# A sparse-expert block whose router reads raw rows, with its adaptive sums placed elsewhere

## The chip, the cores and the metric

The kernel runs on one core of one Trainium2 chip. The metric is the device time of one execution in microseconds (us). The core has five engines that run their own instruction lists side by side and meet at semaphores: TensorE (PE in the profile; PEld is its weight load), VectorE (DVE), ScalarE (ACT), GpSimd (POOL) and SyncE (SP), which here issues most transfers. Each list is executed in order, so an instruction that waits holds back everything behind it on its engine.

## What is computed

Two blocks over 256 tokens of width 1024, in float32. The first is a mixer of three branches followed by a layer of experts; the second is four further layers, whose norms are modulated by adaptive rows (a vector `c` times a matrix plus a bias). The change lies in the first block and in the part of the adaptive rows that is computed during it. The expert layer:

```python
h = rms_norm(x, norm_ffn)                       # x * rsqrt(mean(x*x) + 1e-6) * norm_ffn
lg = h @ w_rg + b_rg;  grp = argmax(lg)         # 4 groups
le = (h @ w_re + b_re)[group grp]               # 8 experts in the group
top_p, top_i = top_k(softmax(le), 2)
gate = top_p / sum(top_p) * softmax(lg)[grp]
x = x + sum over both: gate * (silu(h @ w_eg[e]) * (h @ w_eu[e])) @ w_ed[e]
```

## The kernel before, in words

The program goes stage by stage; the end of a stage is a barrier of all engines. The first block is `hybrid_block` (norm, projections, `delta_rule`, `sparse_attention`, `mix_out`), then `moe_block`, which is `route` (L1386) and `experts` (L1903); `second_block` follows. Matrices are multiplied as high and low halves: ScalarE rounds a weight piece to the high half (`Stream.lift`, L276), VectorE subtracts it for the low half (`Stream.lower`, L286), TensorE makes three products (`product`, L314 to L316). SyncE sends piece n when the piece that had its slot has been lowered (`Stream.send`, L254). The experts' weights go through five slots of 1 MB.

`route` in its order before. SyncE: the norm's gain as 128 full rows, four small loads of the router's weights and biases, three weight pieces, three column loads for the adaptive rows; then, after the logits, bias rows. TensorE first sums the adaptive rows over the partitions: 16 products with a single column of ones, each behind one stir (L322, a dummy product), then turns the normed rows (L1456), makes the logits (L1465, 16 products of 36 columns), sums three half rows of 512 columns (L1353), stirs eight times, waits for the picked group, makes the ranks (L1475, L1478), stirs eight times, and gathers the tokens of each group with a permutation matrix (L1488: for each of eight column blocks the high and the low part in a bank of its own), then the tokens that overflow a group (L1495), then turns the permutation (L1502) and gathers the factors (L1506). ScalarE squares the rows (L1515), rounds the normed rows (L1519), copies half of the turned rows (L1521). VectorE norms the rows with the gain (L1547, that is why everything waits for the gain and the root of GpSimd, L1448), adds the biases (L1568), picks the group by some eight tiny steps, goes on to both experts, and only then waits for the ranks (L1585) and builds the permutation (L1589); then come the weights, the flag of overflow, the merge of the adaptive columns (L1333 to L1337) and the copies of the low halves (L1611). Row merges (`SiteRow.merge`, L1366) each wait for a bias load that overwrites the summed row; the last of them, whose sum and load follow the factors, is the last work of the stage.

`experts`: every engine first reads the flag (`first_of`, L1664), then runs 32 experts; at the end of each, `turn` waits for the product (L1953) and `down` waits for the low half of the hidden rows (L2073). `mix_out`: after the last branch TensorE turns the merged rows in two halves of eight (L3176); the second half waits for the merge of VectorE (L2290).

## Time and profile before

| what | value |
|---|---|
| time, median of 3 runs (lowest, highest) | 2376.83 us (2376.19, 2380.12) |
| span of the profiled execution | 2380.9 us |
| busy: TensorE, its weight load, VectorE, ScalarE, GpSimd | 95%, 80%, 76%, 48%, 6% |
| `route`: first instruction of TensorE to first product of the experts | 434.49 to 484.66 us |
| experts: first product to the turn of the last expert | 484.66 to 1032.22 us |

A row in order of time has the start, the duration, the engine, the line, output and inputs, and in brackets how long the engine sat idle before it and what released it. A float32 product stands as two records (so x16 is eight products), a product of rounded halves or a transposition as one. PEclk is the share of full speed that TensorE's clock was granted: 1.00 is 2.4 GHz and 0.50 is 1.2 GHz.

### The profile page before, as it was taken

How to read it: one execution, taken by the hardware profiler on the slowest of the kernel's cores; microseconds unless marked ns; L12 is line 12 of the kernel's file. 1: busy time of each engine (PE TensorE's matmuls, PEld its weight loads, DVE VectorE, ACT ScalarE, POOL GpSimd, SP SyncE). 2: the span in 40 equal slices, each digit the busy share in tenths (PEclk: the TensorE clock that was granted, in tenths of full speed). 3: DMA queues.
4: the chain of work that ended last, by engine and by line, in shares of the span. 5: the costliest groups of instructions: out<-in, count | busy, mean ns of one | idle time of the engine just before them, and what ended most of it. 6: DMA issues, size and time to landing. Idle time of an engine off the chain costs nothing. (4 is left out here: it accounts for less than half of the span.)

```text
span 2380.9 us, 30361 instructions
## 1 busy us (share of the span) xinstructions
PE 2265.6 (95%) x11981; PEld 1913.7 (80%) x11981; DVE 1813.5 (76%) x2133; ACT 1150.8 (48%) x1197; POOL 132.0 (6%) x229
## 2 busy tenths in 40 slices
PE   7999888999999999989999989999998999898997
PEld 7888677878888888878788887888987888797886
DVE  6887686478888888866788777887796888777545
ACT  4443244367767676744443254432653434364332
POOL 2000100000000000000111000110001111000000
PEclk9999988899999999999999999999999999999999
DMA  8844552489999999964699634996543898344662
GB/s 299 283 124 131 174 176 89 114 300 373 370 356 371 356 369 363 364 211 156 180 376 366 220 125 134 371 371 221 174 136 124 283 376 313 121 143 154 191 193 71
DMA packets 347057, 572.51 MB, mean 240 GB/s; under 512 B 68128, under 2 KB 181280, under 8 KB 346912
## 3 DMA queue, kind: packets, MB, share of 16 engines
q1 hardware_dynamic: 326176, 495.02, 61.5%
q0 software_dynamic: 20736, 75.51, 8.4%
q8 instruction: 97, 1.59, 0.3%
q14 instruction: 48, 0.39, 0.1%
HBM read 569.39 MB, written 1.05 MB: 240 GB/s over the span
## 5 line engine op out<-in xcount | busy, mean ns | idle before, releaser
L286 DVE TENSOR_TENSOR st_lo<-st_raw,st_hi 128x2048 fp32r<-128x2048 f32 (+1 forms) x195 | 441.0, 2267 | 117.5 <-ACT st_hi L276 117.2
L286 DVE TENSOR_TENSOR es_lo<-es_raw,es_hi 128x2048 fp32r<-128x2048 f32 x192 | 429.3, 2286 | 75.9 <-ACT es_hi L276 74.6
L276 ACT CAST st_hi<-st_raw 128x2048 fp32r<-128x2048 f32 (+1 forms) x195 | 368.4, 1892 | 232.5 <-PE ps L316 157.4
L314 PE MATMUL ps<-st_hi,sb_h_hi 128*128 128x512 f32 (+1 forms) x1232 | 462.9, 376 | 15.7 <-DVE sb_h_lo L1139 7.9
L316 PE MATMUL ps<-st_hi,sb_h_lo 128*128 128x512 f32 (+1 forms) x1232 | 453.1, 368 | 0.0
L315 PE MATMUL ps<-st_lo,sb_h_hi 128*128 128x512 f32 (+1 forms) x1232 | 452.9, 368 | 0.0
L276 ACT CAST es_hi<-es_raw 128x2048 fp32r<-128x2048 f32 x192 | 357.6, 1910 | 52.5 <-DMA es_raw<-in_w_expert_up_dram 25.5
L314 PEld LDWEIGHTS ps<-st_hi,sb_h_hi 128*128 128x128 f32 x1232 | 234.1, 190 | 58.4 <-issue 13.0
L316 PEld LDWEIGHTS ps<-st_hi,sb_h_lo 128*128 128x128 f32 x1232 | 233.9, 190 | 38.7
L315 PEld LDWEIGHTS ps<-st_lo,sb_h_hi 128*128 128x128 f32 x1232 | 234.4, 190 | 35.4
L314 PE MATMUL ps<-es_hi,moe_hg_hi 128*128 128x512 f32 x512 | 205.7, 402 | 5.1 <-PEq L61 5.1
L315 PE MATMUL ps<-es_lo,moe_hg_hi 128*128 128x512 f32 x512 | 202.6, 396 | 0.0
L316 PE MATMUL ps<-es_hi,moe_hg_lo 128*128 128x512 f32 x512 | 202.5, 395 | 0.0
L276 ACT CAST hs_hi<-hs_raw 128x1024 fp32r<-128x1024 f32 (+2 forms) x86 | 86.4, 1010 | 156.1 <-PE ps L316 90.1
L1190 DVE SCALAR_TENSOR_TENSOR t_ada<-t_aw,c,t_ada 128x1024 f32<-128x1024 f32 x126 | 156.7, 1279 | 0.4 <-DMA t_aw<-in_ada_w_dram 0.4
L286 DVE TENSOR_TENSOR hs_lo<-hs_raw,hs_hi 128x1024 fp32r<-128x1024 f32 (+2 forms) x86 | 100.7, 1177 | 54.2 <-ACT hs_hi L276 54.1
L314 PE MATMUL ps<-st_hi,t_hid_hi 128*128 128x512 f32 x352 | 140.4, 399 | 1.4 <-DVE t_hid_lo L1162 1.4
L316 PE MATMUL ps<-st_hi,t_hid_lo 128*128 128x512 f32 x352 | 137.2, 390 | 0.0
L315 PE MATMUL ps<-st_lo,t_hid_hi 128*128 128x512 f32 x352 | 137.0, 389 | 0.0
L314 PEld LDWEIGHTS ps<-es_hi,moe_hg_hi 128*128 128x128 f32 x512 | 96.4, 188 | 28.6 <-issue 6.6
L316 PEld LDWEIGHTS ps<-es_hi,moe_hg_lo 128*128 128x128 f32 x512 | 96.2, 188 | 23.6
L315 PEld LDWEIGHTS ps<-es_lo,moe_hg_hi 128*128 128x128 f32 x512 | 96.6, 189 | 22.0
(690 smaller groups left out, 3769.0 us busy)
## 6 DMA issues: line engine op xcount, KB each, us to landing
st_raw<-in_ffn_w_in_dram SPq DMA_DIRECT2D x176, 512.0 KB, 6.7
t_aw<-in_ada_w_dram POOLq DMA_DIRECT2D x144, 512.0 KB, 7.0
es_raw<-in_w_expert_gate_dram SPq DMA_DIRECT2D x64, 1024.0 KB, 8.2
es_raw<-in_w_expert_up_dram SPq DMA_DIRECT2D x64, 1024.0 KB, 7.4
es_raw<-in_w_expert_down_dram SPq DMA_DIRECT2D x64, 1024.0 KB, 7.3
st_raw<-in_ffn_w_out_dram SPq DMA_DIRECT2D x44, 1024.0 KB, 9.1
fb_aw<-in_ada_w_dram SPq DMA_DIRECT2D x39, 512.0 KB, 5.8
hs_raw<-in_w_in_dram SPq DMA_DIRECT2D x36, 512.0 KB, 7.3
```

The costliest lines, as they stand in the source:

```text
L276: act.copy(p.at(self.hi[:, m % self.held, :]), p.at(self.raw[:, n % self.slots, :])).then_inc(self.high, 1)
L286: dve.tensor_tensor(p.at(self.lo[:, m % self.held, :]), p.at(self.raw[:, n % self.slots, :]), p.at(self.hi[:, m % self.held, :]).bitcast(F ...
L314: pe.matmul(out, a_hi, b_hi, start=start, stop=False, skip_group_check=True)
L315: pe.matmul(out, a_hi, b_lo, start=False, stop=False, skip_group_check=True)
L316: return pe.matmul(out, a_lo, b_hi, start=False, stop=stop, skip_group_check=True)
L1190: op = dve.scalar_tensor_tensor(at, aw[:, m % 4, :], k.c[:, kb:kb + 1], at, ALU.mult, ALU.add)
```

## The change

Routing works on the raw rows: TensorE turns `X` itself from the stage's start; the root (1/rms, still from GpSimd) multiplies the logits per token, and the norm's gain is folded into the router's weights beforehand (a product on VectorE in `mix_out`) and into the gathered columns, where a partition is a feature. High and low parts are gathered into one bank and split again. Permutation and ranks come right behind the group's choice, ahead of the choice of experts. The factors are gathered as rounded halves. The small loads go to the start of `delta_rule`; the three weight pieces are the first loads of `route`. The stirs, except two, are gone; the single-column sums stand behind the logits and behind the ranks. The row sums go to `mix_out` (between the two halves of the turns, with a wait for ScalarE's copy) and to the end of `experts`; their biases are added on one partition by accumulating transfers of GpSimd ahead of the sums. The flag and the column merge go to experts 2 and 3, the reading of the flag to expert 8 on VectorE and ScalarE, to the end on TensorE and SyncE.

```diff
 
-    def sums(self, pe, stirs=0):
+    def sums(self, pe, a):
         pe.wait_ge(self.ada.added, self.ada.total)
-        for i in range(16):
-            stir(self.k, pe, 0, stirs)
-            last = pe.matmul(self.psum[:, i:i + 1], self.ada.thirds[i // 8][:, i % 8 * P:(i % 8 + 1) * P],
...
         @block.sync
         def _(sp):
-            with nc.allow_non_contiguous_dma("small vectors"):
-                sp.dma_start(gain[:], rows(A["norm_ffn"][0])).then_inc(q["gained"], 16)
-                for dst, src in smalls:
-                    sp.dma_start(dst, src).then_inc(q["small"], 16)
             S.send(sp, lent)
-            mod.load(sp)
+            sp.wait_ge(q["squared"], NT)
+            S.send(sp, lent + 1)
             sp.wait_ge(q["logits"], 1)
-            for c in range(2):
-                mine_row.load(sp, c)
-            next_row.load(sp, 0)
-            sp.wait_ge(q["low"], NT)
-            S.send(sp, S.slots)
-            next_row.load(sp, 1)
+            S.send(sp, S.slots + 1)
...
-            mod.sums(pe, 1)
-            for t in range(NT):
-                pe.wait_ge(q["normed"], t + 1)
+            for t in range(NT):
                 for i in range(8):
-                    last = pe.transpose(ps[:, 2 * t + i // 4, i % 4 * P:(i % 4 + 1) * P], h[:, t, i * P:(i + 1) * P],
+                    last = pe.transpose(ps[:, 2 * t + i // 4, i % 4 * P:(i % 4 + 1) * P], X[:, t, i * P:(i + 1) * P],
                                         k.ident[:])
                     if i % 4 == 3:
...
-            pe.wait_ge(q["small"], 16 * len(smalls))
+            stir(k, pe, 5, 2)
...
             last.then_inc(q["logits"], 1)
-            for c in range(2):
-                mine_row.sum(pe, c)
-            next_row.sum(pe, 0)
-            stir(k, pe, 0, 8)
+            M.site.sums(pe, 0)
...
             last.then_inc(q["ranked"], 1)
-            stir(k, pe, 0, 8)
+            M.site.sums(pe, 1)
             pe.wait_ge(q["high"], NT)
             pe.wait_ge(q["low"], NT)
             pe.wait_ge(q["placed"], 1)
-            for n, (w, i) in enumerate(jobs):
-                if n >= 4:
-                    pe.wait_ge(q["g_hi" if w == 0 else "g_lo"], n // 2 - 1)
+            for i in range(8):
+                if i >= 4:
+                    pe.wait_ge(q["g_lo"], i - 3)
+                for w in range(2):
+                    for t in range(NT):
+                        last = pe.matmul(ps[:, i % 4, :], (h_hi, h_lo)[w][:, t, i * P:(i + 1) * P],
+                                         perm[:, t, 0:NG, :].rearrange("p j s -> p (j s)"), start=w == t == 0,
+                                         stop=w == 1 and t == NT - 1)
+                last.then_inc(q["gathered"], 1)
+            for j in range(NJ):
                 for t in range(NT):
-                    last = pe.matmul(ps[:, n % 4, :], (h_hi, h_lo)[w][:, t, i * P:(i + 1) * P],
-                                     perm[:, t, 0:NG, :].rearrange("p j s -> p (j s)"), start=t == 0, stop=t == NT - 1)
-                last.then_inc(q["gathered"], 1)
...
+                    last = pe.transpose(ps[:, 4 + j // 2, j % 2 * T + t * P:j % 2 * T + (t + 1) * P],
+                                        perm[:, t, j, :].bitcast(F32), k.ident[:])
+            last.then_inc(q["turned_perm"], 1)
             for c in range(2):
                 for w in range(2):
-                    pe.wait_ge(q["g_hi" if w == 0 else "g_lo"], 7 + c)
+                    pe.wait_ge(q["g_lo"], 5 + 2 * c + w)
...
             pe.wait_ge(q["weighted"], 1)
...
+                    last = pe.matmul(turned_fac[:, j], perm[:, t, j, :], halves[:, t], start=t == 0, stop=t == NT - 1)
             last.then_inc(q["turned_perm"], 1)
-            pe.wait_ge(next_row.merged, 1)
-            next_row.sum(pe, 1)
...
             for t in range(NT):
-                act.wait_ge(q["normed"], t + 1)
-                act.copy(h_hi[:, t, :], h[:, t, :]).then_inc(q["high"], 1)
                 act.wait_ge(q["turned"], 2 * t + 1)
                 act.copy(hT[:, 0:4, t * P:(t + 1) * P], ps[:, 2 * t, :].rearrange("p (k s) -> p k s", k=4)
                          ).then_inc(q["copied0"], 1)
+            for t in range(NT):
+                act.wait_ge(q["rooted"], t + 1)
+                act.activation(h_hi[:, t, :], X[:, t, :], ACT.Copy, scale=ss[:, t:t + 1]).then_inc(q["high"], 1)
+            S.lift(act, 3)
             act.wait_ge(q["chosen"], 1)
             act.activation(ex[:], ex[:], ACT.Exp).then_inc(q["raised"], 1)
-            S.lift(act, 1)
-            for n, (w, i) in enumerate(jobs):
...
+            for i in range(8):
+                act.wait_ge(q["gathered"], i + 1)
+                act.activation(M.hg_hi[:, 0:NG, i, :], ps[:, i % 4, :].rearrange("p (j s) -> p j s", j=NG), ACT.Copy,
+                               scale=k.wgain[:, i:i + 1]).then_inc(q["g_hi"], 1)
             act.wait_ge(q["turned_perm"], 1)
             act.copy(M.permT[:].rearrange("p j t -> p (j t)"), ps[:, 4:6, :].rearrange("p b n -> p (b n)"))
+            for n in range(4):
+                act.wait_ge(q["late_done"], n + 1)
+                act.copy((M.hg_hi, M.hg_lo)[n % 2][:, NG, n // 2 * 4:n // 2 * 4 + 4, :].rearrange("p k s -> p (k s)"),
+                         ps[:, n, :])
...
-            dve.wait_ge(q["gained"], 16)
-            for t in range(NT):
-                dve.wait_ge(q["rooted"], t + 1)
-                dve.scalar_tensor_tensor(h[:, t, :], X[:, t, :], ss[:, t:t + 1], gain[:], ALU.mult, ALU.mult
-                                         ).then_inc(q["normed"], 1)
-            for t in range(NT):
                 dve.wait_ge(q["turned"], 2 * t + 2)
                 dve.tensor_copy(hT[:, 4:8, t * P:(t + 1) * P], ps[:, 2 * t + 1, :].rearrange("p (k s) -> p k s", k=4)
                                 ).then_inc(q["copied1"], 1)
             for t in range(NT):
                 dve.wait_ge(q["high"], t + 1)
-                dve.tensor_tensor(h_lo[:, t, :], h[:, t, :], h_hi[:, t, :].bitcast(F32), ALU.subtract
-                                  ).then_inc(q["low"], 1)
+                dve.scalar_tensor_tensor(h_lo[:, t, :], X[:, t, :], ss[:, t:t + 1], h_hi[:, t, :].bitcast(F32), ALU.mult,
+                                         ALU.subtract).then_inc(q["low"], 1)
...
             dve.wait_ge(q["logits"], 1)
-            after(dve.tensor_tensor(lt[:], ps[:, 4, 0:NT * 36].rearrange("p (t n) -> p t n", t=NT),
-                                    br[:].unsqueeze(1).to_broadcast([P, NT, 36]), ALU.add))
+            for t in range(NT):
+                op = dve.scalar_tensor_tensor(lt[:, t, :], logit(t), ss[:, t:t + 1], br[:], ALU.mult, ALU.add)
...
+            dve.wait_ge(q["ranked"], 1)
+            after(dve.tensor_tensor(cum[:], ranks[:, 0:NT, :], pick[:], ALU.mult))
+            after(dve.tensor_reduce(b1[:], cum[:], AX.X, ALU.add))
+            dve.tensor_scalar(rk[:, :, 0:NG], cum[:], -1.0, None, ALU.add)
+            after(dve.tensor_scalar(rk[:, :, NG:].rearrange("p t o -> p (t o)"), b1[:], -1.0 - P, None, ALU.add))
+            dve.tensor_tensor(perm[:].rearrange("p t j s -> p (t j) s"), slots[:].unsqueeze(1).to_broadcast([P, NT * NJ, P]),
+                              rk[:].rearrange("p t j -> p (t j)").unsqueeze(2).to_broadcast([P, NT * NJ, P]),
+                              ALU.is_equal).then_inc(q["placed"], 1)
...
+            def lower(i):
+                dve.wait_ge(q["g_hi"], i + 1)
+                dve.scalar_tensor_tensor(M.hg_lo[:, 0:NG, i, :], ps[:, i % 4, :].rearrange("p (j s) -> p j s", j=NG),
+                                         k.wgain[:, i:i + 1], M.hg_hi[:, 0:NG, i, :].bitcast(F32), ALU.mult,
+                                         ALU.subtract).then_inc(q["g_lo"], 1)
+            dve.tensor_scalar(M.count[:, 0, :], ranks[:, NT, :], float(P), None, ALU.is_gt)
+            lower(0)
             after(first(mine[:], m2[:], two[:], NE))
...
+            lower(1)
...
+            after(dve.tensor_tensor(one[:], one[:], two[:], ALU.add))
+            after(dve.tensor_copy(halves[:, :, 0, :], one[:]))
+            dve.tensor_tensor(halves[:, :, 1, :], one[:], halves[:, :, 0, :].bitcast(F32), ALU.subtract
+                              ).then_inc(q["weighted"], 1)
+            for i in range(3, 8):
+                lower(i)
             S.lower(dve, 1)
...
             dve.wait_ge(q["turned_perm"], 1)
-            dve.tensor_copy(M.late_perm[:], ps[:, 6, 0:T])
-            dve.tensor_copy(M.fac[:].rearrange("p j e -> p (j e)"), ps[:, 6, T:T + NJ * NE])
-            next_row.merge(dve, 1)
-
-
-def late_programs(k, A, M, st, kept_sums):
+            dve.tensor_copy(M.late_perm, turned_late)
+            dve.wait_ge(q["turned_perm"], 2)
+            after(dve.tensor_copy(M.fac[:], turned_fac[:, :, 0, :]))
+            dve.tensor_tensor(M.fac[:], M.fac[:], turned_fac[:, :, 1, :], ALU.add)
...
     def first_of(eng):
 
+        eng.wait_ge(flagged, 1)
         any_late = eng.value_load(M.flags[0:1, 0:1], min_val=0, max_val=1)
...
                     turn(e - 1)
+                if e == N:
+                    for c in range(2):
+                        last = pe.matmul(ps[:, c, :], k.ones[:], k.gates[:, 1, c * BANK:(c + 1) * BANK], start=True, stop=True)
+                    last.then_inc(row_summed, 1)
+                    found = first_of(pe)
...
+            act.wait_ge(row_summed, 1)
+            act.activation(k.gates[:, 1, :], ps[:, 0:2, :].rearrange("p c n -> p (c n)"), ACT.Identity,
+                           bias=k.ones[:, 0:1])
             keep(NG - 1)
             late_scalar(act, found)
...
+            def flag():
+                after, fl = Chain(dve, flag_step), M.count[:, 1, 0:2]
+                after(dve.tensor_reduce(fl[:, 0:1], M.count[:, 0, :], AX.X, ALU.add))
+                after(dve.tensor_tensor(M.count[:, 0, :], M.count[:, 0, :], M.count[:, 2, :], ALU.mult))
+                after(dve.tensor_reduce(fl[:, 1:2], M.count[:, 0, :], AX.X, ALU.add))
+                after(dve.tensor_scalar(fl[:, 1:2], fl[:, 1:2], float(NE), None, ALU.mult))
+                dve.tensor_copy(M.flags[:], fl).then_inc(flagged, 1)
             for e in range(N + 1):
+                if e == 2:
+                    flag()
+                if e == 3:
+                    M.site.merge(dve)
+                if e == NE:
+                    found = first_of(dve)
...
         def _(sp):
             sp.dma_start(B.gbias[:], rows(A["b_gate"][0, 0:1024])).then_inc(gb.bias_landed, 16)
             mod.load(sp)
+            B.site.load(sp)
+            with nc.allow_non_contiguous_dma("small vectors"):
+                for dst, src in router_loads(k, A):
+                    sp.dma_start(dst, src).then_inc(B.router_landed, 16)
             weave(sending(sp, gb.g, 0), more.fetching(sp, add_at))
...
         def _(sp):
             S.send(sp, len(S.pieces))
+
+        @block.gpsimd
+        def _(pool):
+            pool.dma_start(mine[0:1, :], bias[0, 0:1, 2048:3072], accum_op=ALU.add).then_inc(biased[0], 16)
+            pool.wait_ge(ada.added, ada.total)
+            pool.dma_start(ada.thirds[2][0:1, :], bias[0, 1:2, 2048:3072], accum_op=ALU.add).then_inc(biased[1], 16)
+            pool.wait_ge(biased[1], 16)
...
+                if i == 3:
+                    pe.wait_ge(biased[0], 16)
+                    for c in range(2):
+                        last = pe.matmul(ps[:, 6 + c, :], k.ones[:], mine[:, c * BANK:(c + 1) * BANK], start=True, stop=True)
+                    last.then_inc(row_summed, 1)
+                    pe.wait_ge(row_taken, 1)
...
+                if n == 2:
+                    act.wait_ge(row_summed, 1)
+                    act.activation(mine, ps[:, 6:8, :].rearrange("p c n -> p (c n)"), ACT.Identity, bias=k.ones[:, 0:1]
+                                   ).then_inc(row_taken, 1)
...
+                if c == 0:
+                    dve.wait_ge(B.router_landed, 16 * len(router_loads(k, A)))
+                    dve.tensor_tensor(k.wr[:], k.wr[:], k.wgain[:].unsqueeze(2).to_broadcast([P, 8, 36]), ALU.mult)
```

## Rows read from the trace of the kernel before

**Rows 1.** Head of the page: span of the profiled execution
```profile
span 2380.9 us, 30361 instructions
```

**Rows 2.** Windows: stretch, length, busy of PE, PEld, DVE, ACT, POOL; clock; DMA
```profile
434.40:446.20 11.80, 11.71 (x64) 11.74 (x65) 2.79 (x4) 3.23 (x5) 1.45 (x4) 0.59 0.74 193
...
484.60:488.20 3.60, 3.54 (x9) 2.83 (x10) 3.53 (x2) 3.07 (x2) 0.00 (x0) 0.56 0.38 119
...
490.00:590.00 100.00, 100.00 (x447) 81.20 (x446) 84.33 (x47) 70.82 (x48) 0.00 (x0) 1.00 1.01 366
```

**Rows 3.** TensorE in order of time, routing: start, duration, line, [idle before <- releaser]
```profile
434.49 0.46 PE L322 MATMUL ps<-ident 128*128 128x128 f32 x2 [1.03 <-PEq L61]
...
443.37 0.43 PE L1321 MATMUL ps<-ones,third 128*128 128x1 f32 x2
...
449.66 3.95 PE L1465 MATMUL ps<-rt_wr,es_raw 128*128 128x36 f32 x32
...
453.44 4.52 PE L1353 MATMUL ps<-gates,ones 128*128 128x512 f32 x6
...
460.17 0.59 PE L1478 MATMUL ps<-rt_pick,ones 128*128 128x4 f32 x4
...
463.18 0.69 PE L1488 MATMUL ps<-rt_perm,rt_h_hi 128*128 128x512 f32 x2 [0.53 <-DVE rt_perm L1589]
...
466.91 0.73 PE L1488 MATMUL ps<-rt_perm,rt_h_lo 128*128 128x512 f32 x2 [1.21 <-DVE moe_hg_lo L1611]
...
474.27 1.29 PE L1502 MATMUL ps<-ident,rt_perm 128*128 128x128 f32 x10 [0.26 <-DVE gates L1366]
...
475.39 2.30 PE L1506 MATMUL ps<-rt_one,rt_perm 128*128 128x8 f32 x20
...
484.66 0.79 PE L314 MATMUL ps<-es_hi,moe_hg_hi 128*128 128x512 f32 x1 [5.08 <-PEq L61]
```

**Rows 4.** ScalarE in order of time, routing
```profile
435.53 1.04 ACT L1515 ACTIVATE es_raw<-X 128x1024 f32<-128x1024 f32 x1
...
449.05 0.58 ACT L1521 COPY es_raw<-ps 128x512 f32<-128x512 f32 x1 [0.17 <-PE ps L1456]
```

**Rows 5.** VectorE in order of time, routing
```profile
439.29 2.48 DVE L1547 SCALAR_TENSOR_TENSOR es_raw<-X,rt_ss,rt_gain 128x1024 f32<-128x1024 f32 x2 [2.44 <-DMA rt_gain<-in_norm_ffn_dram]
...
453.75 0.23 DVE L1568 TENSOR_TENSOR rt_lt<-ps,rt_br 128x72 f32<-128x72 f32 x1 [0.88 <-PE ps L1465]
...
460.86 0.17 DVE L1585 TENSOR_TENSOR rt_cum<-ps,rt_pick 128x8 f32<-128x8 f32 x1 [2.90 <-PE ps L1478]
...
461.54 1.49 DVE L1589 TENSOR_TENSOR rt_perm<-rt_slots,rt_rk 128x1280 fp32r<-128x1280 f32 x1
...
482.75 0.69 DVE L1366 SCALAR_TENSOR_TENSOR gates<-ps,gates 128x512 f32<-128x512 f32 x1 [4.20 <-DMA gates<-in_ada_b_dram]
```

**Rows 6.** TensorE and windows in the mixing output stage ahead of routing
```profile
404.64 1.04 PE L3176 MATMUL ps<-ident,fb_merged 128*128 128x128 f32 x8
...
408.79 1.53 PE L3176 MATMUL ps<-ident,fb_merged 128*128 128x128 f32 x8 [3.12 <-DVE fb_merged L2290]
...
409.00:413.00 4.00, 4.00 (x16) 3.37 (x15) 3.40 (x5) 2.12 (x3) 0.00 (x0) 0.57 0.05 19
```

**Rows 7.** TensorE, then VectorE, at the last expert
```profile
1032.22 0.60 PE L1953 MATMUL ps<-ident,moe_idle 128*128 128x128 f32 x4
...
1033.48 0.69 DVE L2073 TENSOR_TENSOR ex_hid_lo<-ps,ex_hid_hi 128x512 fp32r<-128x512 f32 x1
```

**Rows 8.** One line: the flag read on TensorE's queue
```profile
L1664 PEldq TENSOR_LOAD <-moe_flags x1: 487/487/487, 483.8 to 483.8; - x1
```

**Rows 9.** SyncE at 442 us; SyncE and ScalarE at the delta rule
```profile
442.67 8.07 SPq L1315 DMA_DIRECT2D cols<-in_ln_g_dram  x1
...
112.52 1.36 SPq L254 DMA_DIRECT2D hs_raw<-in_w_in_dram  x1
...
135.76 0.64 ACT L276 CAST hs_hi<-hs_raw 128x560 fp32r<-128x560 f32 x1
```

181 lines of the change are left out of this document (71 added, 110 removed).

## The prediction, made before the changed kernel was run

> **What bounds the kernel now.** The page comes first: TensorE is busy 95% of a span of 2380.9 us [rows 1], so time can go only where TensorE waits, where it works for nothing, or where its clock is low. The windows show such a place. In the experts, 490 to 590 us, TensorE is busy throughout at full clock; between 434.4 and 446.2 it is busy too, but at a granted clock of 0.59, and the experts' first 3.6 us stand at 0.56 [rows 2]. The third view, TensorE in order of time, says what this work is: stirs and single-column sums [rows 3], which nobody ahead of the experts needs. What the stage waits for is found in the order of time of VectorE: it norms the rows only at 439.29, released by the gain's transfer; its logits come at 453.75; then the permutation's chain begins only at 460.86, because TensorE did row sums and stirs before the ranks; and the stage's last work is a row merge at 482.75 that had waited 4.20 us for a bias [rows 5]. From the stage's first product at 434.49 to the experts' first at 484.66 [rows 3] is 50.2 us, nearly all of it one chain. So the sum is the new chain from 434.5 on, link by link.
>
> **Turns, squares, copies.** The turns of raw rows need neither root nor gain, and start at 434.5. Eight turns take 1.04 us at full clock [rows 6], so sixteen end at 436.5. ScalarE's second square runs from 435.53 for 1.04 us [rows 4]; with its readout it is free at 436.7. Its two copies of turned rows, 0.58 us each [rows 4], stand right behind, at 437.2 and 437.8. VectorE's copies fall in between.
>
> **Logits.** 32 records in 3.95 us at mostly full clock [rows 3], 0.12 us each; at the lower clock a record of this kind takes 0.21 us (two single-column ones 0.43, row 443.37) [rows 3], so 6.8 us. They start at 437.3. The stirs mixed with single columns did not hold the clock: 0.59 over 11.8 us [rows 2] is 2.1 us at full and the rest at half. The logits are 36 columns wide; I expect the fall inside or right behind them, and set their end at 441.5 (ends 441.0 and 444.2). VectorE's low rows (one product with a scalar of 1.24 us each, half of row 439.29 [rows 5]) end near 441.2 and hold nothing. Saved to here: 453.6 less 441.5, 12 us.
>
> **Pick, ranks, permutation.** The pick is eight tiny steps 0.2 us apart, the first of them the row at 453.75 [rows 5]: done at 443.2. The first eight sums stand ahead of the ranks, sixteen records: 3.4 us low, 1.9 full, so the ranks start at 444.9, not at 443.2. This is a new wait of 1.7 us: picked is queued behind them. The ranks are ten records; four of them take 0.59 us at full clock [rows 3], so 1.2 us, or 2.1 us low: 447.0. The permutation follows at once (460.86 to 463.03 before [rows 5], 2.2 us): 449.2. The second eight sums run meanwhile on TensorE and end at 450.4: they hold the gather by another 1.2 us. Gather at 450.4; before at 463.18 [rows 3], 12.8 us later.
>
> **Gather.** 32 products of 512 columns; in the experts 447 products fill 100 us [rows 2], 0.224 us each, so 7.2 us. Before there was one stall, 1.21 us [rows 3], since VectorE did flags and merges first; these go away, but the splits now need both ScalarE (0.6) and VectorE (0.7) in series for each bank, and VectorE has the choice of experts (1.7 us) ahead of the first split and some twelve tiny steps between the first three. By that list TensorE waits 0.5 to 1.5 us in all. If the clock is low at its start, half the pace costs up to 1.7 us more. I take 9.5 us (ends 8.5 and 13.7, the latter all at half pace): end at 459.9.
>
> **Tail.** Ten turns 1.29 us [rows 3], eight products for overflow 1.8 us, then ten factor records instead of twenty: half of 2.30 us [rows 3], 1.2 us: 464.2. VectorE lowers one weight piece (2.3 us) and is ready just then; two tiny steps: 464.6. ScalarE's four copies behind the permutation's end near 463.6. The last row sum, its bias load and the 4.20 us behind it [rows 5] are gone. The next stage's first product came 1.2 us after the last merge (483.44 to 484.66); 0.49 us of it is the flag's read [rows 8] with its bookkeeping, so I take 0.3: 464.9. **Routing saves 484.66 - 464.9 = 19.8 us.**
>
> **The experts' start.** Before, 3.6 us at clock 0.56 [rows 2] lost 3.6 x 0.44 = 1.6 us. The idle time ahead shrinks from 5.08 us [rows 3] to about 1, but the factor records are as narrow as before, so I count under half, 0.7 saved (0 to 1.6).
>
> **mix_out.** The two row sums are four passes of 512 columns each: 4.52 us for three of them at a mixed clock [rows 3], 1.7 us for two at full clock. They lie in the 3.12 us in which TensorE waits for VectorE's merge [rows 6]: 405.5 to 407.3, ScalarE's copy of 1024 (1.04) to 408.4, the merge comes at 408.7. So the new wait for ScalarE, behind which all turns and products of the output stand, is covered by 0.3 us only; uncovered it costs 1 us. On the other side eight turns took 1.53 us and not 1.04 after that idle time, and the stretch 409 to 413 ran at 0.57 [rows 6], 1.7 us lost: if the work in the gap keeps the clock up, 1.9 us come back. I take 0.5 saved (-1.0 to 1.9). The gain's product on VectorE, near 0.4 us for 288 columns, lies between two of TensorE's chunks where VectorE is idle.
>
> **End of the experts.** The turn of the last expert starts at 1032.22 and VectorE's half is done at 1034.17 [rows 7]: a gap of some 1.4 us for 1.7 us of row sums, and then the flag's read, 0.49 us with 0.2 behind it [rows 8]. Cost 0.8 us (0.2 to 1.2). Flag and merge are some eleven tiny steps, 2 us of VectorE in experts 2 and 3. It is busy 84% there [rows 2], with weights split ahead, so 0.2 us (0 to 2).
>
> **Sum.** 19.8 + 0.7 + 0.5 - 0.8 - 0.2 = 20.0 us. Against the profiled execution 2380.9 becomes 2360.9. The median of the runs shown is 4.1 us under that span (this execution was slower than any of them), and nothing suggests that the change's part scales: 2376.8 - 20.0 = 2356.8 us.
>
> **What comes first at delta_rule.** Eight small loads now stand on SyncE's queue ahead of the weight piece issued at 112.52. That piece is first read by ScalarE at 135.76 [rows 9]; with about 3 us to land, 20 us of cover. The nearest price of a small load is 8.07 us [rows 9], but behind three weight pieces that were still in transit, which at 2.9 us a piece explains it. So I take nothing lost; the other end is the rival below.
>
> **Rivals.** *Clock up all the way* (0.15): the turns of dense 128 columns carry it through logits and sums. Then logits end at 441.0, sums at 442.9, ranks at 444.1, permutation and gather at 446.3, gather's end at 455.2, first product 460: 24.9 us saved in routing, with the other terms 25: 2352. For it: the clock was full at 434.5 and during the gather. Against: stirs and sums at 434.4 to 446.2 took it to 0.59 [rows 2].
>
> *Clock down early* (0.17): it falls in the turns, as it fell 2.1 us into the old stage. Logits end at 444.2, first sums 447.6, ranks 449.7, second sums 453.1, gather's end 462.6 to 464.5, first product 467.6 to 469.5: 15 to 17 us saved: 2360 to 2362. The removed stirs speak for it. The Trainium skill, page "TensorE: Matmul & The Clock Gate", section "Part 1: The HAM clock gate", has the low clock as the default and activity as what lifts it, which speaks against taking stirs out. By that rule alone this rival would be the likeliest; the rows show that stirs mixed with single-column sums did not keep the clock up either, so it stays the second.
>
> *The experts give it back* (0.05): transfers are at 366 GB/s and a share of 1.01 there [rows 2]; if the weight stream and not TensorE sets the pace, starting early only turns into waits. Then only the slots filled ahead come early: five pieces at 2.9 us (1.05 MB at 366 GB/s) were sent by 459 and would now be sent by 441; the stream behind them starts with the first product and runs at its own pace, of which I allow it to take back half, 10 us: 2367. Against: TensorE shows no idle time there, and SyncE sends only when a slot was lowered.
>
> *Slower* (0.03): the eight loads of small elements each take what the dearest took, 8.07 us: 65 us on SyncE, against 20 us of cover. TensorE then loses 45 us in the delta rule, and the time is near 2400. It decides from 20 us cover plus 20 us saved, 40 us for eight loads, 5 us each. The Trainium skill, "DMA: Bandwidth & Descriptors", section "Specifications", puts line rate at elements of 512 B or more, and these have 4 to 128 B; no row here prices such loads by themselves.
>
> *It does not do what it says* (0.05): a wait in the new order that I misread (the third lifted piece, landed near 445 at 2.9 us a piece, stands ahead of ScalarE's first gathered copy) takes 5 to 15 us; still faster, 2362 to 2372.
>
> **Chances.** The forecast has 0.55. A measurement of this kernel tells about 0.2%, 4.8 us, from no change. Faster by more holds in the first three cases and most of the last: 0.93. Within: 0.03. Slower: 0.04. The range for 8 in 10 runs from the full-clock case with its extra terms, 2350, to the early fall with the unknown costs of mix_out and the experts, 2364.
>
> **What would show it.** After: turns at the start of routing with no wait; logits near 7 us in; the ranks directly behind the sums, the gather directly behind the second sums (if it waits for the permutation instead, the clock was up); no load of a bias at the end; first expert product 30 us after the stage's start; TensorE's wait for the last low half gone but for a read of the flag; no wait in the delta rule for a weight piece. I am wrong if the gather takes over 11 us, if the third lift delays the copies, or if the experts show waits for weights.

## The result and the profile after

The changed kernel takes 2363.52 us (median; 2357.58 to 2366.01), the kernel before beside it 2378.47 us (2376.19 to 2386.61): a ratio of 0.9924, 95% interval 0.9899 to 0.9949. It is faster, by more than 0.2%, and inside the range of 2350 to 2364, but only half a microsecond from its slow end; the forecast was 2356.8. One of fifty later executions of the kernel before fell in a slow state, 2858.70 us at a granted clock of 0.741, and is left out of all that follows. The profiled span fell from 2380.9 us [rows 1] to 2364.2 us, 16.7 us instead of 20.0. The page's head:

```profile
span 2364.2 us, 30212 instructions
PE 2257.6 (95%) x11911; PEld 1906.7 (81%) x11911; DVE 1808.2 (76%) x2130; ACT 1156.1 (49%) x1201; POOL 133.4 (6%) x231
```

TensorE in routing, in order of time, the answer to [rows 3]:

```profile
433.91 1.94 PE L1415 MATMUL ps<-ident,X 128*128 128x128 f32 x16 [1.03 <-PEq L61]
436.61 3.76 PE L1424 MATMUL ps<-wr,es_raw 128*128 128x36 f32 x32 [0.31 <-ACT es_raw L1472]
440.20 2.92 PE L1319 MATMUL ps<-ones,gates 128*128 128x1 f32 x16
442.98 0.57 PE L1430 MATMUL ps<-rt_pick,upto 128*128 128x4 f32 x2
...
445.12 3.55 PE L1319 MATMUL ps<-ones,third 128*128 128x1 f32 x16
448.53 1.20 PE L1443 MATMUL ps<-rt_perm,rt_h_hi 128*128 128x512 f32 x2
...
458.70 1.25 PE L1449 MATMUL ps<-ident,rt_perm 128*128 128x128 f32 x10
...
461.64 1.18 PE L1462 MATMUL ps<-rt_halves,rt_perm 128*128 128x16 f32 x10
463.59 0.47 PE L313 MATMUL ps<-es_hi,moe_hg_hi 128*128 128x512 f32 x1 [0.77 <-PEq L61]
```

No row but the logits' and the next stage's has idle time ahead of it: the stage is one run of TensorE work, 29.68 us long where it was 50.17 us. What is left of its waits is hidden in slow work, as the windows of the same stretches tell (granted clock third from the right):

```profile
433.90:440.00 6.10, 5.78 (x51) 5.60 (x51) 3.38 (x6) 5.45 (x9) 1.51 (x5) 1.00 0.80 253
440.00:443.00 3.00, 3.00 (x21) 3.00 (x20) 2.24 (x10) 2.18 (x2) 0.00 (x0) 0.65 1.03 397
443.00:453.00 10.00, 10.00 (x38) 9.03 (x39) 5.01 (x21) 6.15 (x6) 0.00 (x0) 0.50 0.68 253
...
454.50:463.60 9.10, 8.33 (x48) 7.11 (x47) 7.91 (x16) 6.68 (x12) 0.00 (x0) 1.00 0.01 2
463.60:467.20 3.60, 3.60 (x16) 2.92 (x17) 3.60 (x2) 3.16 (x2) 0.00 (x0) 1.00 0.79 290
```

The clock (1.00 is 2.4 GHz, 0.50 is 1.2 GHz) fell with the first single-column sums and came back half way through the gather; the experts start at 1.00, where they had 0.56 [rows 2]. The moment of the fall differs from execution to execution of this same kernel: in a second trace of it (the experiment "again" below) the first group of sums still ran at full clock and the fall came right behind it, which brings the ranks 1.0 us earlier:

```profile
440.97 1.93 PE L1319 MATMUL ps<-ones,gates 128*128 128x1 f32 x16
...
444.81 3.55 PE L1319 MATMUL ps<-ones,third 128*128 128x1 f32 x16
```

VectorE, the answer to [rows 5]. The permutation's chain waits 2.88 us, now for the ranks, which stood behind the first sums; there is no wait for a gain or a bias. Its next wait, 2.14 us, is for ScalarE's first gathered copy:

```profile
441.75 0.17 DVE L1511 TENSOR_TENSOR rt_pick<-rt_pick,rt_b 128x8 f32<-128x8 f32 x1
...
445.37 0.17 DVE L1524 TENSOR_TENSOR rt_cum<-ps,rt_pick 128x8 f32<-128x8 f32 x1 [2.88 <-PE ps L1432]
...
446.04 1.49 DVE L1528 TENSOR_TENSOR rt_perm<-rt_slots,rt_rk 128x1280 fp32r<-128x1280 f32 x1
...
451.34 0.75 DVE L1541 SCALAR_TENSOR_TENSOR moe_hg_lo<-ps,wgain,moe_hg_hi 128x512 fp32r<-128x512 f32 x1 [2.14 <-ACT moe_hg_hi L1482]
```

The output mix, the answer to [rows 6]: the row sums stand between the two groups of turns, and the wait for the merge is 1.49 us instead of 3.12. The second group takes 1.06 us, not 1.53, and the window that ran at 0.57 runs at 1.00:

```profile
406.45 1.88 PE L3180 MATMUL ps<-gates,ones 128*128 128x512 f32 x4
409.83 1.06 PE L3173 MATMUL ps<-ident,fb_merged 128*128 128x128 f32 x8 [1.49 <-DVE fb_merged L2264]
```

```profile
409.00:413.00 4.00, 3.17 (x18) 2.82 (x19) 3.63 (x7) 2.51 (x4) 0.00 (x0) 1.00 0.26 101
```

At the experts' end, the answer to [rows 7]: from the last turn to the last expert's third product it is 2.09 us with the sums and the flag's read in between; before, it was 2.10, 1.49 of them idle. In the kernel before:

```profile
1034.32 0.47 PE L314 MATMUL ps<-es_hi,ex_hid_hi 128*128 128x512 f32 x1 [1.49 <-DVE ex_hid_lo L2073]
```

and in the changed one:

```profile
1011.30 0.60 PE L1905 MATMUL ps<-ident,moe_idle 128*128 128x128 f32 x4
1011.74 1.88 PE L1944 MATMUL ps<-gates,ones 128*128 128x512 f32 x4
1013.39 0.47 PE L313 MATMUL ps<-es_hi,ex_hid_hi 128*128 128x512 f32 x1
```

### Where the time went, by marks

A mark is the first or last record of TensorE on a named tile. Between marks, in us:

| stretch | before | changed | changed, repeated |
|---|---|---|---|
| gdn_z projection to delta rule (no edited line) | 14.16 | 15.72 | 15.75 |
| delta rule to mix_out | 278.41 | 278.37 | 276.43 |
| mix_out, merged turns to end | 28.83 | 27.31 | 27.41 |
| its end to ranks | 26.11 | 10.09 | 9.09 |
| ranks to gather | 3.60 | 5.55 | 5.47 |
| gather | 9.01 | 10.33 | 9.83 |
| gather's end to first expert product | 12.47 | 4.73 | 4.73 |
| to the first expert's turn | 15.51 | 14.07 | 14.08 |
| first turn to end of last turn (32 experts) | 532.65 | 534.24 | 534.26 |
| experts' last product to the scatter's end | 4.09 | 5.42 | 4.10 |

So the edited stretches saved 20.5 (routing), 1.4 (experts' start) and 1.5 (mix_out); the experts lost 1.6, evenly, 0.05 us in each. That is 21.8 us: 23.4 us won, 1.6 given back. The other 5.1 us of the difference to 16.7 lie in stretches that show no edited line, each a difference of about 1 to 2.5 us, and where I looked a short stretch of low clock. The one before the delta rule, in the windows of the kernel before:

```profile
96.00:100.00 4.00, 4.00 (x18) 3.29 (x19) 2.42 (x2) 1.98 (x2) 0.00 (x0) 1.00 1.05 399
```

and of the changed one:

```profile
96.00:100.00 4.00, 4.00 (x12) 3.11 (x12) 2.42 (x2) 0.42 (x2) 0.00 (x0) 0.57 1.07 395
```

### The profile page after: what moved, and what is told of

It is laid out like the page before. It is cut to its first block and busy times, and to the rows that moved or that the text cites. A ratio compares the mean times of both kernels' runs of the same rounds, so it can differ in the third digit from the quotient of the medians.

```text
span 2364.2 us, 30212 instructions
## 1 busy us (share of the span) xinstructions
PE 2257.6 (95%) x11911; PEld 1906.7 (81%) x11911; DVE 1808.2 (76%) x2130; ACT 1156.1 (49%) x1201; POOL 133.4 (6%) x231
```

## The experiments

All were timed against the kernel before in the same job; its medians there were 2382.43 us (with the first, second, third and fourth kernel below), 2381.80 (the next four), 2380.91 (the next three) and 2381.38 (the last). A saving is the difference to the median of its own job. Intervals are 95%.

**The changed kernel again**, without an edit, as the measure for the others.

> The changed kernel as it is, unedited, to see how far two executions of one kernel differ at the same places. In its first trace it was 21.1 us ahead of the kernel before at the first expert product and 16.7 us at the end; 1.6 us of the difference were lost evenly over the experts, 1.3 us at the scattering after them, some 2.5 us in the later layers, and 1.6 us in a projection ahead of every edited line. Theory A (the clock's level at places the change does not touch is chance): these losses move or vanish here, only the even 1.6 us in the experts stays. Theory B (the change causes them): all come back at the same places. Median 2359 to 2365, ratio 0.991 to 0.994.

2364.32 us (2361.98 to 2365.50), ratio 0.9923 (0.9908 to 0.9938): 18.1 us saved. This median lies just outside the range of the forecast. Of the losses away from the edits the one ahead of the delta rule came back (15.75 us) and the one at the scatter vanished (4.10 us), so neither theory holds for all of them; the even 1.6 us in the experts stayed. The stage itself took 28.10 us and not 29.68, because the clock fell later, and that is the measure of what one trace can tell about it. The three runs of before that the forecast was made on, 2376.19 to 2380.12 us, lay low; eleven here gave 2378.66 to 2387.88.

**The single-column sums left out** (the later site's columns lack them).

```diff
-            M.site.sums(pe, 0)
             pe.wait_ge(q["picked"], 1)
...
-            M.site.sums(pe, 1)
             pe.wait_ge(q["high"], NT)
```

> The sixteen single-column sums of routing are left out (so the adaptive columns of the next block lack them and the output changes). Theory: in the changed kernel they held the ranks by 1.0 us and the gather by 1.0 us; without them the ranks start when the pick is made, the gather when the permutation is placed: 2 us off the stage, 29.7 us down to about 27.7. If the clock matters more than the queue, the gather still starts at half speed (there is even less work ahead of it), and nothing beyond the 2 us comes. Rival: the sums are free fillers of waits, 0 us.

2360.97 us (2358.93 to 2363.28), ratio 0.9910 (0.9895 to 0.9925). What stands behind the sums appears as waits:

```profile
442.30 0.59 PE L1430 MATMUL ps<-rt_pick,upto 128*128 128x4 f32 x2 [1.61 <-DVE rt_pick L1510]
...
447.01 1.19 PE L1442 MATMUL ps<-rt_perm,rt_h_hi 128*128 128x512 f32 x2 [2.42 <-DVE rt_perm L1527]
```

The ranks start no earlier (9.09 us behind mix_out's end, as in the repeated run), the gather 0.75 us earlier. So the sums do lie in TensorE's waits for VectorE, at 0.8 us of the path up to the gather. The whole stage takes 26.93 us, 1.2 us less than in the repeated run and 2.75 less than in the first trace, against 2 us expected. The clock fell here too, to 0.50, with TensorE idle, so it is not the sums alone that bring it down.

**Eight stirs in the place of each group of sums** (again no sums). A stir is a dummy product of 128 columns.

```diff
-            M.site.sums(pe, 0)
+            stir(k, pe, 5, 8)
...
-            M.site.sums(pe, 1)
+            stir(k, pe, 5, 8)
```

> The same sixteen records twice, but with 128 columns (eight stirs each) and not a single one (sums left out, so the adaptive columns lack them). Theory that the narrowness of the sums puts the clock down: it stays at 1.00 through ranks and gather, the gather takes 7.3 to 9 us and not 10.2, the ranks start 1 us and the gather 2 us earlier: 4 to 5 us off the stage. Rival: the logits with their 36 columns have already put it down, the stirs lift it again only by the second set: 1 to 3 us. If neither, 0.

2361.33 us (2355.27 to 2364.70), ratio 0.9914 (0.9897 to 0.9930). The clock stays at 1.00:

```profile
437.00:443.60 6.60, 6.08 (x54) 5.91 (x54) 5.33 (x18) 4.44 (x4) 0.00 (x0) 1.00 1.04 392
443.60:453.50 9.90, 8.73 (x34) 5.94 (x35) 7.38 (x29) 7.20 (x11) 0.00 (x0) 1.00 0.41 151
```

The Trainium skill, page "TensorE: Matmul & The Clock Gate", section "Part 1: The HAM clock gate", has activity as what lifts the clock; this pair of runs agrees in part, 1.00 with the stirs against 0.65 and 0.50 with the sums. It agrees only in part because the profile counts TensorE as busy without a break over the sums too (3.00 of 3.00 us and 10.00 of 10.00), so its busy time does not tell the two apart. The gather starts 3.60 us behind the ranks and not 5.55, but takes 9.84 us: TensorE waits in it, 0.26 to 0.49 us at a time, for low halves of VectorE. These in turn stand behind ScalarE, whose first gathered copy comes 2.75 us behind the gather's start, since the third lift and a table load stand ahead of it:

```profile
443.02 1.91 ACT L275 CAST es_hi<-es_raw 128x2048 fp32r<-128x2048 f32 x1 [0.77 <-DMA es_raw<-in_w_expert_up_dram]
444.95 1.28 ACT L1480 ACT_TABLE_LOAD   x1
446.24 0.21 ACT L1480 ACTIVATE rt_ex<-rt_ex 128x10 f32<-128x10 f32 x1
446.36 2.40 ACT L1483 ACTIVATE moe_hg_hi<-ps,wgain 128x512 fp32r<-128x512 f32 x4
```

The stage takes 26.33 us, 1.8 us less than in the repeated run and 3.35 less than in the first trace: under the 4 to 5 us that were expected, since the gather was to take 7.3 to 9 us and takes 9.84.

**The permutation moved back behind both choices of experts**, all else as changed.

> Ranks and permutation on VectorE stand behind both choices of experts again, as before the change; all else is the changed kernel. VectorE sat idle for 2.88 us between the masked logits and the ranks in the changed kernel. My theory: this part of the change is worth nothing, for the first choice (1.7 us) fits into that idle time; with the second choice (0.8 us) it is 2.5 us and still fits, 0 us (-0.3 to 0.3). Rival, the intent of the change: the permutation comes 2 to 2.5 us later and the gather with it.

2362.28 us (2356.95 to 2366.35), ratio 0.9916 (0.9898 to 0.9933). The stage takes 29.72 us, against 29.68 and 28.10 in the two traces of the changed kernel, and the gather starts 5.55 us behind the ranks, against 5.55 and 5.47. VectorE takes its steps for both experts while TensorE sums, and still waits for the ranks:

```profile
440.95 0.17 DVE L1538 TENSOR_TENSOR rt_cum<-ps,rt_pick 128x8 f32<-128x8 f32 x1 [0.98 <-PE ps L1432]
```

As was expected, this part of the change is worth nothing that can be seen by itself.

**The root back ahead of the turns**, by a product on VectorE; gain, sums and order as changed.

```diff
+                pe.wait_ge(q["normed"], t + 1)
...
-                    last = pe.transpose(ps[:, 2 * t + i // 4, i % 4 * P:(i % 4 + 1) * P], X[:, t, i * P:(i + 1) * P],
+                    last = pe.transpose(ps[:, 2 * t + i // 4, i % 4 * P:(i % 4 + 1) * P], sq[:, t, i * P:(i + 1) * P],
...
+                dve.tensor_scalar(sq[:, t, :], X[:, t, :], ss[:, t:t + 1], None, ALU.mult).then_inc(q["normed"], 1)
```

> The changed kernel with the root back ahead of the turns: VectorE writes rows times root (two products of 1.24 us) and TensorE turns these; gain folded into the weights, permutation order and sums stay. Theory (raw rows matter because the turns need no root): the turns start behind the second square, the root and one product, 3 to 5 us after the stage's start, and the first expert product comes 3 to 5 us later than in the changed kernel, with at least half of it lost again to a low clock where TensorE stood idle. Rival (the other parts make the gain and the root lay hidden behind sums): under 1 us.

2369.16 us (2365.49 to 2371.90), ratio 0.9952 (0.9938 to 0.9967): 12.6 us saved where the changed kernel saves 18.1; the ranks come 15.42 us behind mix_out's end instead of 9.09 to 10.09. Behind the idle time of 4.10 us the turns take nearly twice their 1.94 us. The edit also sends one weight piece only behind the logits; that is not what is seen, since the stretches from the ranks on (5.55, 9.96 and 4.72 us) are as in the changed kernel.

```profile
437.83 3.68 PE L1414 MATMUL ps<-ident,es_raw 128*128 128x128 f32 x16 [4.10 <-DVE es_raw L1498]
```

**The kernel before without its opening sums and stirs** (the later site's columns lack the sums).

> The kernel before, with only the opening sums and stirs of its routing left out (so the column norm of the later site lacks its sums). Theory (root, gain's transfer and norm bound the turns, not the stirs): the turns start near 6 us into the stage rather than at 0, so only 3 to 6 us of the 12 us saved up to the logits come, and the total gains 3 to 6 us. Rival (TensorE's own sums and stirs are what delayed the turns): 9 to 12 us.

2380.48 us (2375.99 to 2387.79), ratio 0.9997 (0.9983 to 1.0011): nothing. TensorE, relieved, waits for the gain:

```profile
438.80 2.48 DVE L1547 SCALAR_TENSOR_TENSOR es_raw<-X,rt_ss,rt_gain 128x1024 f32<-128x1024 f32 x2 [3.26 <-DMA rt_gain<-in_norm_ffn_dram]
...
440.14 3.67 PE L1456 MATMUL ps<-ident,es_raw 128*128 128x128 f32 x16 [7.98 <-DVE es_raw L1547]
```

The two runs split the 16 to 17 us that are saved ahead of the ranks. The opening work weighs 0.7 us (25.38 against 26.11 to the ranks): it covered a later wait and was no cause, and the 3 to 6 us of the expectation were too much. The root, with its product on VectorE and the slow clock behind the wait, weighs 5.3 to 6.3 us (against the two traces of the changed kernel; in the other traces with its opening the ranks come 9.09 to 11.33 us behind mix_out's end). The gain's transfer adds 3.9: TensorE idles 7.98 us ahead of the turns with both, 4.10 with the root alone. By subtraction some 6 us are left for the row sums, the stirs and the slow clock between turns and ranks; these were not tried one by one.

**A row's tail at the stage's end again**: half a row's sum, its bias (2 KB for each of 128 partitions, 256 KB in all by the trace) and the merge.

```diff
+            sp.wait_ge(q["rowed"], 1)
+            sp.dma_start(k.gates[:, 1, 0:BANK], rows(A["ada_b_2"][0, 1][2048:3072])[:, 0:BANK]).then_inc(q["row_landed"], 16)
...
+            pe.matmul(ps[:, 4, :], k.ones[:], k.gates[:, 1, 0:BANK], start=True, stop=True).then_inc(q["rowed"], 1)
...
+            dve.scalar_tensor_tensor(k.gates[:, 1, 0:BANK], ps[:, 4, :], 1.0, k.gates[:, 1, 0:BANK], ALU.add, ALU.add)
```

> The changed kernel with a row's tail put back behind the permutation's turns: one row sum of 512 columns, the load of half a bias of 2 KB sent behind the last weight piece, and VectorE's merge of both at the stage's end (the merged value is used nowhere). Theory (the tail cost what the trace of before showed, 4.20 us of wait for the bias plus the merges): the first expert product comes 3 to 6 us later. Rival (the load is hidden: it is sent early enough, and only the merge of 0.6 us is seen): under 1 us.

2371.91 us (2366.20 to 2373.25), ratio 0.9962 (0.9947 to 0.9976): 9.9 us saved, 8.2 less than the changed kernel. (The merged value is read by the gate's row sum after all, so it does change the output, not the work.) The first expert product comes 6.1 us later, at the upper end of what was expected, and more is lost behind it. From the gather's end to the experts it is 10.84 us against 4.73, and the experts' start takes 16.31 against 14.07, at a clock of 0.50: the wait is paid twice.

```profile
468.87 0.69 DVE L1576 SCALAR_TENSOR_TENSOR gates<-ps,gates 128x512 f32<-128x512 f32 x1 [5.42 <-DMA gates<-in_ada_b_dram]
```

**The row sum in the output mix left out**, with ScalarE's copy and the wait for it (the gate lacks its summed row).

> The changed kernel without the row sum of the residual gate in the output mix: its four records on TensorE, the wait for ScalarE and ScalarE's copy are left out (so the gate lacks its summed row; the bias is still added). In the changed kernel the row sums fill the time in which TensorE waits for the merge, the granted clock is 1.00 where it was 0.57, and this stretch of the output takes 22.24 us where it took 23.50. Theory (the work in the gap holds the clock, the wait is covered): without it the clock falls again, the output products lose 1.3 to 1.9 us, and the stretch takes 23.5 to 24.1 us. Rival (the clock there is chance, the wait for ScalarE costs its full 1 us): the stretch shrinks to 21.2 to 22.2 us.

2366.50 us (2362.52 to 2368.87), ratio 0.9946 (0.9931 to 0.9960): less work, and 15.3 us saved instead of 18.1. From the merged turns to the stage's end it is 28.93 us against 27.31 and 27.41; the wait is 3.22 us, and the same window falls back to 0.57. The stretch is as clear over all traces: 27.30 to 27.41 us in the eleven with the sums in the gap, 28.83, 28.93 and 29.29 us in the three without.

```profile
408.90 1.43 PE L3174 MATMUL ps<-ident,fb_merged 128*128 128x128 f32 x8 [3.22 <-DVE fb_merged L2264]
```

```profile
409.00:413.00 4.00, 4.00 (x15) 3.41 (x16) 3.50 (x5) 2.12 (x3) 0.00 (x0) 0.57 0.05 18
```

So the sums between the turns keep the clock and are worth 1.5 us; the wait for ScalarE is covered: its copy ends at 409.48, VectorE's merge at 409.68. The other 1.3 us of the 2.8 us lie elsewhere. In its trace the clock of the next stage falls earlier too and the ranks come 11.33 us behind mix_out's end; whether the missing sums cause that was not tried.

**A version of my own: the sums inside the gather**, eight stirs in their old places.

```diff
-            M.site.sums(pe, 0)
+            stir(k, pe, 5, 8)
...
-            M.site.sums(pe, 1)
+            stir(k, pe, 5, 8)
...
+                if i == 4 or i == 6:
+                    M.site.sums(pe, i // 2 - 2)
```

> A whole kernel: dense stirs (eight products of 128 columns) stand in the waits for the pick and for the permutation, and the single-column sums move into the gather, half ahead of the fifth bank and half ahead of the seventh, where TensorE waits for VectorE's halves. Theory (single-column work lets the clock fall; the gather at full clock is bounded by ScalarE and VectorE, whose waits hide the sums): the clock stays at 1.00, the gather starts 3.6 us after the ranks (5.5 in the changed kernel), takes 9.8 to 10.6 us, and the first expert product comes 26.3 to 27.2 us into the stage, 1 to 3 us earlier than in the changed kernel. Rival (the sums there add their 1.9 us in full): 28.2 us, no gain.

2363.33 us (2357.52 to 2367.12), ratio 0.9922 (0.9900 to 0.9944). The clock is 1.00 throughout, the gather takes 11.19 us (9.84 without the sums: 1.35 of their 3.7 us are seen), and from mix_out's end to the first expert product it is 28.70 us, against 30.70 and 29.12: 0.4 to 2.0 us better in the stage, which the total does not show. The first expert product comes 27.68 us into the stage, later than the 26.3 to 27.2 us expected, since the gather is 0.6 us longer than its forecast.

**The same, with the third lift behind the overflow's copies** (`S.lift(act, 2)` ahead of the exponential, `S.lift(act, 3)` last).

> The kernel with the sums in the gather, and ScalarE's third lift (1.9 us, whose piece lands last) behind its copies for the overflow rather than ahead of the exponential. Theory (the lift stands ahead of the first gathered copy, which comes 2.7 us behind the gather's start): the first copy comes some 1.5 us earlier, TensorE waits less ahead of banks five and six, the gather takes 8.8 to 9.5 us, and 0.5 to 1 us is gained on the same kernel without this move. Rival (VectorE's chain of twelve tiny steps and halves is the bound, or the experts wait for the late lift): 0, or a loss up to 1.9 us at the experts' start.

2363.56 us (2357.89 to 2368.38), ratio 0.9921 (0.9898 to 0.9945). The first copy does come 1.4 us earlier (1.61 us behind the gather's start, not 2.99), but the gather takes 11.20 us, not less, where 8.8 to 9.5 were expected: with the sums in its waits TensorE is the bound there. The lift comes due again at the stage's end, TensorE waits 2.26 us for the next stage, the clock is at 0.58 over the 4 us around it, and the two stretches to the first expert's turn lose 1.47 and 1.28 us. The rival of the late lift held.

**A pad of 320 bytes behind the counts.** The change moved the tiles of the experts in memory: the weight tiles, hidden rows and sums began at 32 bytes past a multiple of 64 per partition before, and at a multiple of 64 after it.

```diff
+        M.pad = sb("pad", [P, 80])
```

> The changed kernel with an unused tile of 320 bytes per partition placed behind the counts in the expert block, which brings the tiles behind it back to where they lay before the change. In every kernel with the change the 32 experts take 534.24 to 534.26 us from the first to the last turn, in the kernels without it 532.60 to 532.65, evenly over the experts, in the records of the third product (0.2333 us rather than 0.2275 for some of them). Theory (the place of the operands in memory sets this): 532.6 us again, 1.6 us less in all. Rival (it comes from the smaller share of VectorE or ScalarE work or another thing in the change): 534.25.

2365.21 us (2360.76 to 2365.67), ratio 0.9926 (0.9905 to 0.9946); the 32 experts take 534.40 us. No gain in all. The pad was also the wrong size: the shift that the change made is 288 bytes, since tile sizes are rounded up to 32 bytes, and 320 is itself a multiple of 64, so it left the remainder as the change had made it.

**The kernel with the sums in the gather and a pad of 288 bytes** (`[P, 72]`), which puts these tiles exactly where they lay before. The gathered rows, ahead of the pad, stay where the change put them, 352 bytes lower than before.

> The whole kernel with the sums in the gather and an unused tile of 288 bytes per partition behind the counts. The pad of 320 bytes left the weight tiles, the hidden rows and the sums on multiples of 64 bytes per partition, as in the changed kernel; with 288 bytes they lie exactly where they lay before the change, 32 bytes past such a multiple. Theory (the place of these tiles sets the pace of the third product): the 32 experts take 532.6 us from the first to the last turn instead of 534.26, and the total is 1.6 us under the same kernel without the pad. Rival (it is the gathered rows, which this pad does not move, or no matter of place): 534.2 to 534.4 us.

2361.02 us (2356.84 to 2364.80), ratio 0.9925 (0.9901 to 0.9949). The 32 experts take 533.02 us, 1.24 us less than without the pad; 532.6 were expected. TensorE over 500 us of experts, its records in brackets, in the kernel before:

```profile
500.00:1000.00 500.00, 500.00 (x2227) 406.87 (x2226) 433.43 (x251) 357.64 (x235) 0.00 (x0) 1.00 1.01 365
```

with the sums in the gather and no pad:

```profile
500.00:1000.00 500.00, 500.00 (x2220) 406.15 (x2219) 431.73 (x255) 355.77 (x235) 0.00 (x0) 1.00 1.01 364
```

and with the pad of 288 bytes:

```profile
500.00:1000.00 500.00, 500.00 (x2226) 407.78 (x2225) 432.86 (x256) 356.67 (x235) 0.00 (x0) 1.00 1.01 365
```

Nothing but the pad differs between the last two kernels, so where tiles lie does change the pace, by 1.24 of the 1.6 us. But no simple rule comes out. The sum of the times from each record's start to the next, from the first turn to the last, divides the experts by product:

| kernel | gate and up products, us | down product, us |
|---|---|---|
| before | 346.62 | 168.87 |
| changed | 347.05 | 170.07 |
| changed, pad of 320 bytes | 348.34 | 168.99 |
| sums in the gather | 347.05 | 170.08 |
| sums in the gather, pad of 288 bytes | 346.16 | 169.68 |

The change slowed the down product above all, by 1.20 us. Yet the pad of 288 bytes, with which every tile that this product reads or writes is back at its old place, gives back only 0.40 of them and takes the rest of its gain from gate and up; the pad of 320, which keeps the remainder by 64, gives back nearly all of them and loses as much in gate and up. So the remainder alone does not set the pace of a product, and what does stays open. By its ratio this kernel is no faster than the one without the pad (0.9925 against 0.9922); its median is the lowest of the whole kernels of the study, in a job of its own.

## Why the prediction held, point by point

The mechanism held: the stage lost the waits that were named, in the order that was named. The closeness of the total is partly luck. The terms of the sum were together too small, 23.4 us were won where 20.0 were forecast, and two things that the sum did not have, the pace of the experts and slow stretches elsewhere, took 6.7 us back.

**Routing, forecast 19.8, measured 20.5** (22.1 in the repeated run). In us from the stage's start, forecast and measured: logits start 2.8 and 2.7; picked 8.7 and 8.0; ranks 10.4 and 9.1; gather 15.9 and 14.6; its end 25.4 and 24.9; first product 30.4 and 29.7. Each link is within 1.3 us. The clock fell where it was expected, behind the logits, not ahead (in the repeated run one group of sums later): the rivals of a clock that stays up (29.7 us, not 25.5) and of one that falls in the turns (the logits took 3.76 us, not 6.8) did not occur. The term that was too small is the gather: 10.33 us against 9.5, since its first 5.7 us ran at half pace; the lift and table load ahead of ScalarE's first copy were no bound in that state, and became one at full clock. In the changed kernel that rival did not occur; the run with the stirs shows its mechanism, waits of 0.26 to 0.49 us and not of 5 to 15.

**Experts' start, 0.7 forecast, 1.4 measured.** The idle time shrank to 0.77 us and the clock was at 1.00 from the first product; the halving of the gain for the narrow factor records was too careful. The row-tail run shows the other side: 2.2 us lost behind 5.9 us of idle.

**mix_out, 0.5 forecast, 1.5 measured.** I took a middle between a clock regained and a wait uncovered. The run without the row shows both ends: the clock's 1.5 us are real, the wait costs nothing.

**End of the experts, 0.8 forecast, 0 measured.** The step that failed is the adding up: sums and the flag's read both fitted into the wait for the low half, 2.09 us against 2.10. (The forecast's own terms, 1.7 less 1.4, 0.49 and 0.2, make 1.0 and not 0.8.) **Flag and merge in experts 2 and 3, 0.2 forecast, nothing seen** in their own experts. **Small loads at the delta rule, 0, held:** nine loads (one of them stood there before) hold SyncE from 111.34 to 120.53 and move the weight piece there from 112.52 [rows 9], yet the stretch takes 278.37 us against 278.41; the 3% rival did not come.

```profile
111.34 3.26 SPq L1314 DMA_DIRECT2D cols<-in_ada_b_dram  x2
...
120.53 0.58 SPq L253 DMA_DIRECT2D hs_raw<-in_w_in_dram  x1
```

**What the sum left out.** First, the experts' pace: 1.6 us, of which 1.24 went with a shift of the tiles and the rest stays open; no view of the kernel before showed it. Second, the baseline: the forecast subtracts from 2376.8, and the kernel before measures 2380.9 to 2382.4 in the medians of four jobs, forty-nine runs; that is 4.1 to 5.6 of the 6.7 us by which the median misses. The saving measured in the repeated run is 18.1 us against 20.0; by the first job's own medians, of four runs each, it is 15.0. Third, the short stretches of low clock away from every edit. By the marks of all fourteen traces several stretches take one of two values: gdn_z to the delta rule 14.1 or 15.7, the last layer 304.7 to 305.0 or 306.6 to 307.6. The latter is high in seven of the twelve traces with the changed order and in neither of the two without it; the former in eight of twelve and in neither. Whether the change makes the high value likelier, or two traces are too few to tell, stays open.

## What to carry to other kernels

When a stage is one chain through several engines, take out what the first link waits for (here root and gain) and not the filler work on top of it: the filler removed alone gave nothing, the root put back cost 5.5 us. Put useful work into a wait only where the wait ends on another engine, and price it with the clock: here four wide products in a gap kept it at 1.00 and paid 1.5 us, while it fell to 0.50 over the single-column sums or right behind them. And when tiles are added or dropped ahead of a long steady loop, measure that loop again: a pad of 288 bytes alone changed 534.26 us of it by 1.24.

## What the chip did that was not expected

- The pace of a steady stream of 512-column products depends on where tiles lie: a pad of 288 bytes took the 32 experts from 534.26 to 533.02 us with nothing else changed. With the weight, hidden and sum tiles 32 bytes past a multiple of 64 bytes per partition the experts took 532.60 to 533.02 us in three kernels, at a multiple of 64 they took 534.24 to 534.40 us in all others; but the single products do not follow that remainder (the down product took 168.87 and 169.68 us in the first case, 168.99 and 170.07 in the second), so it is a correlation and no rule.
- In two executions of the same kernel the clock fell at different places of the stage, over the first sums or behind them: the same sixteen records took 2.92 and 1.93 us, the stage 29.68 and 28.10.
- Leaving out the row sum made the stretch 1.5 us slower: behind the idle gap of 3.22 us the clock is 0.57 over 4 us.
- A wait of 5.42 us for half a bias row (256 KB by the trace), issued 1.22 us behind a weight piece of 1 MB, cost 8.3 us by the marks: 6.1 in itself and 2.2 by the clock behind it.
